# A decoder trunk of two layers on one core: SyncE's program written out per layer, with the next layer's first loads in the tail of the layer

## What is computed

```python
for i in range(DEPTH):
    mix, sg, sd, sc = _mixer(_rmsnorm(h, norm_mix[i]), w_in[i], ..., w_out[i], s_gla[i], s_gdn[i], s_conv[i])
    h = h + mix
    h = h + _peer(_rmsnorm(h, norm_ffn[i]), w_peer_q[i], peer_sub_keys[i], peer_u[i], peer_v[i])
    gate = jax.nn.sigmoid(_rmsnorm(h, norm_ple[i]) @ w_ple_gate[i] + b_ple_gate[i])
    h = h + gate * (p[i] @ w_ple_proj[i])
y = _rmsnorm(h, norm_final)
```

## Time and profile before

| | us |
|---|---|
| median of 3 runs | 2510.52 (2509.81 to 2511.47) |
| the profiled execution | 2502.38 |
| its span, first to last instruction | 2500.8 |
| TensorE busy | 2142.7 (86%) |
| VectorE busy | 1447.2 (58%) |
| GpSimd busy | 1316.3 (53%) |
| ScalarE busy | 692.5 (28%) |

### The profile page before, as it was taken

The page is one execution under the profiler, slowest core; times in us unless marked ns, Lnnn a source line. Parts: engine busy times, 40 slices in busy tenths (PEclk is TensorE's granted clock), DMA queues, the critical chain, the costliest instruction groups (busy, mean ns, idle before and its releaser), DMA issues.

```text
span 2500.8 us, 22276 instructions
## 1 busy us (share of the span) xinstructions
PE 2142.7 (86%) x6952; PEld 1219.3 (49%) x6952; DVE 1447.2 (58%) x3602; ACT 692.5 (28%) x1641; POOL 1316.3 (53%) x1387
## 2 busy tenths in 40 slices
PE   7998989889888877789779998898897798787797
PEld 5667664444334433335456686654443344333354
DVE  1445336566676766676315463365666767666763
ACT  3323223222223331223223232222222223312232
POOL 2013136676777777777100131366677777777771
PEclk9998999999889999989889989999899999888998
DMA  7320079999999999999373201799999999999993
GB/s 226 105 83 24 28 272 341 405 404 406 409 409 409 409 409 409 409 407 406 125 205 101 87 20 51 272 344 404 406 406 409 409 409 405 409 409 409 409 392 134
DMA packets 260983, 761.96 MB, mean 305 GB/s; under 512 B 26973, under 2 KB 91413, under 8 KB 260861
## 3 DMA queue, kind: packets, MB, share of 16 engines
q0 software_dynamic: 188480, 686.97, 70.1%
q1 hardware_dynamic: 72380, 73.50, 9.2%
HBM read 751.66 MB, written 8.72 MB: 304 GB/s over the span
## 4 chain that ended last, share of the span: by engine, by line
PE 46%; DMA 28%; POOL 11%; DVE 7%; issue 5%; ACT 2%; SPq 0%; DVEq 0%; ACTq 0%; POOLq 0%
PE ps L1690 45%; DMA arena<-in_peer_u_dram,idx_u 27%; POOL arena L722 6%; POOL arena L716 5%; DVE arena L1294 3%; DMA wring<-in_w_in_dram 1%; ACT arena L1101 1%; PE ps L1706 0%; DVE xn L1630 0%; DVE wgt L1302 0%; ACT xn L999 0%; DVE arena L1568 0%; DVE arena L1555 0%; DMA h<-in_x_sample_dram 0%; DVE arena L1571 0%
## 5 line engine op out<-in xcount | busy, mean ns | idle before, releaser
L1690 PE MATMUL ps<-arena 128*128 128x512 f32 (+5 forms) x3808 | 1423.4, 529 | 271.5 <-ACT arena L1101 249.5
L1690 PEld LDWEIGHTS ps<-arena 128*128 128x128 f32 (+3 forms) x3808 | 671.6, 204 | 972.5 <-issue 903.2
L1294 DVE CUSTOM_DVE_ANT_0 arena<-arena,ps 128x1024 f32<-128x1024 f32 x640 | 779.7, 1221 | 528.4 <-DMA arena<-in_peer_u_dram,idx_u 508.3
L722 POOL DMA_INDIRECT arena<-in_peer_v_dram,idx_u x640 | 608.0, 950 | 297.0 <-PE ps L1690 160.3
L716 POOL DMA_INDIRECT arena<-in_peer_u_dram,idx_u x640 | 607.8, 950 | 273.5 <-issue 174.5
L1690 PE MATMUL ps<-aT,wring 128*128 128x320 f32 (+2 forms) x1344 | 371.6, 432 | 12.2 <-ACT aT L1008 4.9
L1094 ACT ACTIVATE gelu<-hid 128x4 f32<-128x4 f32 x160 | 32.9, 206 | 1103.3 <-DVE hid L1294 1103.2
L1690 PEld LDWEIGHTS ps<-aT,wring 128*128 128x128 f32 x1344 | 254.5, 197 | 135.6 <-issue 45.4
L1690 PE MATMUL ps<-wring,aT 128*128 128x256 f32 x960 | 224.6, 388 | 3.9 <-ACT aT L1066 2.6
L1690 PEld LDWEIGHTS ps<-wring,aT 128*128 128x128 f32 x960 | 182.0, 193 | 51.9 <-issue 25.7
L1101 ACT ACTIVATE arena<-ident,wgt 128x128 f32<-128x128 f32 x512 | 163.4, 390 | 73.8 <-DVE wgt L1302 72.4
(11 more groups left out here) (297 smaller groups left out, 1355.3 us busy)
## 6 DMA issues: line engine op xcount, KB each, us to landing
wring<-in_w_in_dram SPq DMA_DIRECT2D x28, 1024.0 KB, 5.8
wring<-in_w_peer_q_dram SPq DMA_DIRECT2D x18, 1024.0 KB, 11.8
arena<-in_peer_u_dram,idx_u POOLq DMA_INDIRECT x640, 13.1
arena<-in_peer_v_dram,idx_u POOLq DMA_INDIRECT x640, 13.1
wring<-in_w_out_dram SPq DMA_DIRECT2D x8, 1024.0 KB, 5.3
wring<-in_w_ple_gate_dram SPq DMA_DIRECT2D x8, 1024.0 KB, 17.6
arena<-in_state_gdn_dram POOLq DMA_DIRECT2D x2, 2048.0 KB, 18.5
out_dram<-arena POOLq DMA_DIRECT2D x2, 2048.0 KB, 11.9
```

The costliest lines, as they stand in the source:

```text
L722: pool.indirect_dma_start(vrow[:, n % G, :], None, v_l, bass.IndirectOffsetOnAxis(ap=at, axis=0)).then_inc(v_loaded[n % G], 16)
L1294: dve.tensor_tensor_reduce(out=urow[:, n % G, :], in0=urow[:, n % G, :], in1=x_bank, scale=1.0, scalar=0.0, op0=ALU.mult, op1=ALU.add, acc ...
L1690: return pe.matmul(out, lhsT, rhs, start=start, stop=stop, skip_group_check=True)
```

## The change

SyncE's loop over the layers becomes a Python loop, so that its instructions are written out twice. The 16 small loads become a function `open_layer(layer)`, in which `hist_rows` now stands ahead of the five small pieces of weights. `load_block` gets the layer as an argument. For layer 0 both are called as before. For layer 1, `open_layer` and block 0 are called at the end of layer 0's program, behind a wait for the last list of indices and for the last use of `urow`; SyncE then waits until these loads have landed, signals the meeting, clears the semaphores as before, and sets the semaphores of those loads again to the values that the other engines will wait for. So that slot 0 of the ring is free by then, the last block of a layer (block 30) goes into slot 1 instead of slot 0 and waits for two more query products.

```diff
+    def ring_slot(n):
+        return 1 if n == len(blocks) - 1 else n % RING
...
-            with sp.Fori(0, DEPTH) as layer:
+            def open_layer(layer):
...
+                sp.dma_start(hist_rows[:, :], state_conv[bass.ds(layer, 1), :, :, :].rearrange(
+                    "o b j c -> (o b j) c")).then_inc(hist_loaded, 16)
                 w_l = w_in[bass.ds(layer, 1), :, :]
...
-                sp.dma_start(hist_rows[:, :], state_conv[bass.ds(layer, 1), :, :, :].rearrange(
-                    "o b j c -> (o b j) c")).then_inc(hist_loaded, 16)
...
+            def load_block(layer, n):
+                t, c = blocks[n]
+                if n == len(blocks) - 1:
+                    sp.wait_ge(q_mm, 1 + 2 * HP)
+                elif n >= B_PQ + RING:
+                    sp.wait_ge(q_mm, 1 + 2 * (n - RING - B_PQ))
+                elif n >= RING:
+                    sp.wait_ge(block_used, n - RING + 1)
+                sp.dma_start(wring[:, ring_slot(n), :, :],
...
+            opening = ((par_loaded, 7 * 16), (ptok_loaded, 48), (hist_loaded, 16),
+                       (small_loaded, 80))
+            for layer in range(DEPTH):
+                if layer == 0:
+                    open_layer(0)
+                    load_block(0, 0)
+
+                for n in range(1, RING):
+                    load_block(layer, n)
...
+                if layer + 1 < DEPTH:
+
+                    sp.wait_ge(idx_ready, NSTEP)
+                    sp.wait_ge(u_free, G + NSTEP * TOPK)
+                    open_layer(layer + 1)
+                    load_block(layer + 1, 0)
+                    for loaded, n in opening:
+                        sp.wait_ge(loaded, 2 * n)
+                    sp.wait_ge(w_loaded[0], 7 * 16)
 
                 sp.drain().then_inc(layer_done, 1)
                 sp.wait_ge(layer_done, (layer + 1) * 5)
                 sp.sem_inc(met, 1)
                 sp.sem_clear(range(first, last + 1))
+                if layer + 1 < DEPTH:
+                    for loaded, n in opening:
+                        sp.sem_inc(loaded, n)
+                    sp.sem_inc(w_loaded[0], 16)
                 sp.drain().then_inc(cleared, 1)
...
             def arrived(n):
-                pe.wait_ge(w_loaded[n % RING], 16 * (n // RING + 1))
+                pe.wait_ge(w_loaded[ring_slot(n)], 16 * (n // RING + 1))
```

More of the change, by code:

```diff
@@ L526, in _ @@
                              ).then_inc(small_loaded, 16)
-                sp.dma_start(hist_rows[:, :], state_conv[bass.ds(layer, 1), :, :, :].rearrange(
-                    "o b j c -> (o b j) c")).then_inc(hist_loaded, 16)
[L530 to L541, removed]
+            def load_block(layer, n):
[7 more added lines that the diff above has]
+                sp.dma_start(wring[:, ring_slot(n), :, :],
+                             t[bass.ds(layer, 1), :, c:c + WCOLS].rearrange(
+                                 "o (k p) n -> p (o k) n", p=P)).then_inc(w_loaded[ring_slot(n)], 16)
+            opening = ((par_loaded, 7 * 16), (ptok_loaded, 48), (hist_loaded, 16),
[6 more added lines that the diff above has]
+                    load_block(layer, n)
                 sp.dma_start(gain_row[:, :], row(norm_ffn, layer).to_broadcast([P, D])
@@ L544, in _ @@
                 for n in range(RING, B_PQ + 2 * RING):
-                    load_block(n)
+                    load_block(layer, n)
                 sp.wait_ge(mix_add, 12)
@@ L2176, in embed @@
                         ins = mm(gate_of(i, m), aT[:, k, P * i:P * (i + 1)],
-                                 wring[:, blk % RING, k, :], False, k == KD - 1)
+                                 wring[:, ring_slot(blk), k, :], False, k == KD - 1)
                     if part == 1:
```

## The result

| | before | after |
|---|---|---|
| median of 5 runs, us | 2510.14 (2507.27 to 2511.47) | 2495.78 (2491.96 to 2497.16) |
| the profiled execution, us | 2502.38 | 2493.58 |
| its span, us | 2500.8 | 2492.0 |

The ratio is 0.9946 with a 95% interval of 0.9933 to 0.9959, so 10 to 17 us less of 2510; the medians differ by 14.4. The two profiled executions differ by only 8.8, and single executions of either kernel spread over several microseconds. I therefore read the change in the trace, at the place where it acts: from the end of VectorE's last instruction of layer 0 to TensorE's first product with block 0 of layer 1. I call this stretch the boundary. Before, it is 1276.13 - 1246.15 = 29.98 us.

The account below looks back on a forecast made before the run. Bound mostly by TensorE's products and expert-row gathers; the change acts on 29.8 us of late loads between layers. Opening 13.0 us earlier minus 0.3 for code fetch saves 12.7: 2510.5 - 12.7 = 2497.8 us, range 2495.5 to 2502.5.

Parts of the forecast that it names:

- the branch behind them: After the meeting, TensorE's jump back, 3.885 us and formerly hidden under the wait for `par_rows`, becomes first on the path.
- the tail of layer 0: End of layer 0: early loads disturb nothing, VectorE still ends near 1246; cost zero, 1.3 us either way.
- The boundary: Between the layers: TensorE takes block 0 of layer 1 13.0 us earlier, 12.7 after 0.3 for the code fetch.
- The first transpose: Opening of layer 1: TensorE's first transpose comes at 1251.25 instead of 1252.95, before the 0.3 us fetch allowance.
- my second measure: Layer 0's whole opening, 12.28 us, used for layer 1's: block 0 taken at 1263.5, 12.6 us saved.
- The fetch beside the blocks: After the meeting, code fetches run while blocks 1 to 4 start; 0.3 us lost, bounds 0 and 6.1.
- the rival of 6.1 us: Code fetch behind TensorE's branch delayed by blocks 1 to 4; at the bound 6.9 us saved, 2503.6; chance 0.09.
- Late block 1: Layer 1's opening: block 1 lands last of the loads, 4.6 us lost, 8.1 saved, 2502.4; chance 0.03.
- low clock in the history: TensorE runs layer 1's history and 24-column product at the lower clock; 2.6 us lost, 10.1 saved; chance 0.06.
- late loads: SyncE's meeting waits for loads landing past 1246.2, delaying all engines; over 0.2% slower from about 1264; chance 0.03.
- The rest of the layer moves as a whole: From block 0 to VectorE's last work, layer 1 takes 1217 to 1218 us; the opening's saving lasts within 1.3.
- The other edits cost nothing: Last gate block in slot 1, history issued five places earlier, SyncE's loop written out: no cost either way.

Follow-up runs that it names:

- small_early: The changed kernel, but only the 16 small loads start early and block 0 is issued behind the meeting; boundary 17.39 us, ratio 0.9942 to the kernel before.
- late_open: The changed kernel, but SyncE begins layer 1's loads only after the layer's twelfth gate product; boundary 25.16 us, ratio 0.9989 to the kernel before.
- written_out: The changed kernel with nothing loaded early: SyncE's program written out, layer 1's loads issued after the meeting; boundary 25.09 us, ratio 0.9970 to the kernel before.
- block_early: The changed kernel, but only block 0 starts early and the 16 small loads follow the meeting; boundary 26.32 us, ratio 0.9973 to the kernel before.
- states_held: The kernel before, with GpSimd's 3 MB of state loads waiting until TensorE has used block 0; boundary 18.79 us, ratio 0.9956 to the kernel before.
- three_out: The changed kernel with TensorE's, ScalarE's and VectorE's loops also written out, a drain behind each meeting; boundary 12.16 us, ratio 0.9930 to the kernel before.
- three_again: The kernel with TensorE's, ScalarE's and VectorE's loops also written out, run again beside the changed kernel; median 2488.71 us, boundary 12.11 us, ratio 0.9934.
- after_again: The changed kernel run a second time, unaltered; median 2493.75 us, boundary 15.77 us, ratio 0.9940 to the kernel before.
- pe_out: The changed kernel with TensorE's loop also written out, with a drain behind the meeting; boundary 13.21 us, ratio 0.9933 to the kernel before.

## Why the prediction was right, step by step

The forecast was 2497.8 us (2495.5 to 2502.5), 12.7 saved; measured were 2495.78, so 14.4 saved by the medians and 13.6 by the ratio. The place, the waits and the branch behind them were as predicted; one step, the tail of layer 0, failed, and the agreement of the boundary to a tenth is luck.

- *The boundary.* 12.7 was forecast, 12.70 measured in the first trace. Two terms were off and cancelled, and the next two traces gave 14.2. (The 29.8 us that the prediction gives for the boundary before are 29.98; its sum doesn't use them.) The first transpose was forecast 5.4 us after VectorE's last instruction (1251.25 + 0.3 - 1246.15) and came after 5.00, 4.70 and 4.82. From there to block 0 I took 11.8 us and saw 12.28, 11.07 and 11.01. Layer 0's opening, my second measure, was 12.28. What differs is TensorE's clock over the 24 transposes: 5.33 us of the 12.28, 4.12 and 4.06 of the others.
- *The fetch beside the blocks.* The 0.3 us that I allowed was not there. TensorE's branch took 3.94, 3.64, 3.66, 3.67 and 3.50 us in the kernels where weight blocks were issued behind the meeting (the change three times, small_early, late_open), and 3.89, 3.56, 3.56 and 3.74 where only small loads were (before, written_out, block_early, states_held). So the rival of 6.1 us fell. The Trainium skill ("DMA: Bandwidth & Descriptors", section "Queues, rings and completion order") says that a DMA engine goes round its queues packet by packet; these branches fit with that. By itself that rule doesn't tell how soon a small load is complete: the 2 KB one of block_early took 9.9 us beside the states.
- *Late block 1, low clock in the history, late loads.* None occurred: no wait for `wring`, 4.49 us for the 24-column product in every trace of the change, loads over by 1225. late_open shows the price that the last of these would have had.
- *The tail of layer 0.* This step failed. I forecast that VectorE ends layer 0 near 1246, within 1.3 us; it ended at 1249.30, 0.86 because the last dot product was later, 2.29 because the tail took 38.64 us (1210.66 to 1249.30) instead of 36.35. My 1.3 came from the last products alone. The sixteen expert products and the eight transposes before them also run at either level of the clock, here first in the kernel before, then in the changed one (timeline, and the window with the granted clock):

```profile
1210.82 7.11 PE L1690 MATMUL ps<-arena 128*128 128x512 f32 x16 [2.98 <-ACT arena L1101]
...
1221.83 1.09 PE L1706 MATMUL ps<-ident,xn 128*128 128x128 f32 x8 [1.98 <-DVE xn L1320]
...
1210.00:1215.00 5.00, 4.18 (x10) 2.01 (x11) 1.14 (x4) 3.85 (x9) 0.00 (x0) 1.00 0.04 16
...
1211.67 8.80 PE L1715 MATMUL ps<-arena 128*128 128x512 f32 x16 [2.98 <-ACT arena L1126]
...
1224.37 1.97 PE L1731 MATMUL ps<-ident,xn 128*128 128x128 f32 x8 [1.98 <-DVE xn L1345]
...
1210.00:1215.00 5.00, 3.33 (x5) 1.53 (x6) 0.98 (x5) 4.00 (x9) 0.00 (x0) 0.73 0.23 65
```

  These two groups make up 1.69 and 0.88 us of the 2.29; the last products were 0.27 shorter. The early loads aren't the cause: layer 0's tail took 38.89 in written_out and 38.99 in states_held, which load nothing there, and 36.29 and 36.22 in three_out and three_again, which do; layer 1's tail, in which no kernel loads, shows the same two levels, 36.0 to 36.4 in four traces and 38.2 to 39.0 in the other eight.
- *The rest of the layer moves as a whole.* Too tight. From block 0 to the last dot product, layers took 1177.8 to 1185.2 us over the twelve traces, with no order by kernel. In the pair of profiled executions it is the tails that hide part of the gain (8.8 left of 12.7): they were 2.29 and 2.22 us longer after the change, while the rest came out 0.6 shorter. The span of after_again is only 3.2 us shorter than that of the kernel before, with 14.2 saved at the boundary, because its tails and gathers were 11.8 longer. The kernel before has only one trace, with both tails at the short level, from an execution 8 us under its median.
- *The other edits cost nothing.* No run shows a cost, but they aren't nothing alone: written out, with the history earlier, they shorten the boundary by 4.9 us where the loads stay behind the meeting. In the change these loads are there long before they are needed, so that nothing of this can add to the gain.
- *What the sum didn't see.* It took the whole opening as one piece that had to be early. small_early shows that block 0's early issue brings nothing as long as the small loads are out of its way, and states_held that the crowd of the states, not the late issue alone, cost most of the boundary (11.2 us).

## What to carry to other kernels

Where several loads stand in a row on the chain, the one to move is the one that is small and waited for, ahead of the large transfers that its own consumer sets off; here the first transposes released 3 MB of states onto loads still being issued, and holding those back saved almost as much as starting early. When a wait at the top of a loop goes, look for the jump under it, which becomes the next item on the path: TensorE's is the length of its branch row, VectorE's the gap between its branch row and the next move. And price a stretch by several traces before crediting a few microseconds to an edit: tails moved by 3 us and gathers by 7 here, with no order by kernel.

## What the runs showed of the hardware

- A taken branch at the end of a layer took TensorE 3.50 to 3.94 us in nine kernels and runs, whether or not 1 MB loads were issued beside it; from VectorE's branch to its next move 3.0 us passed in pe_out (1251.7 to 1254.7), of which the branch's own row shows 0.07.
- A load of 2 KB took 9.9 us from issue to release beside 3 MB of state loads; the history's 144 KB took 3.2 us at most in states_held, where they were held.
- After about 3.0 us of idle time the same sixteen products of the tail ran in 7.1 us in some executions and in 8.8 in others, with TensorE's granted clock at 1.00 or below (1.00 in 1210 to 1215 of the kernel before, 0.73 of the changed one). Each level came up with the early loads and without them; what chooses it stays open.
